# A 256-token, four-layer fp32 transformer kernel: the attention gates are applied after the last pair, and the delta rule's base inverse is computed by VectorE instead of GpSimd

## The reference, cut to what matters

```python
for l in range(DEPTH):
    h = rms_norm(x, norm_w[l])
    p = h @ w_in[l]
    qa, ka, va, za, ub, zb, qkv_c, b_c, a_c, zc = _split_cols(p)
    ...
    oa = sliding_window_sink_attention(qa, ka, va, sinks[l]) * jax.nn.silu(za)
    ob = conformer_conv_module(ub, ...) * jax.nn.silu(zb)
    oc = gated_deltanet(qkv_c, b_c, a_c, ...)
    oc = rms_norm(oc, c_onorm_w[l]) * jax.nn.silu(zc...)
    y = jnp.concatenate([oa, ob, oc], axis=-1)
    x = x + y @ w_out[l]
```

```python
lower = jnp.where(strict, jnp.einsum('bhnid,bhnjd->bhnij', kb, kc) * decay, 0.0)
sol = lax.linalg.triangular_solve(lower + eye, rhs, left_side=True, lower=True,
                                  unit_diagonal=True)
```

## Time and profile before

| | us |
|---|---|
| median of 3 runs | 3613.13 |
| lowest, highest | 3611.47, 3616.95 |
| profiled execution | 3615.81 |
| its span (first to last instruction) | 3614.0 |
| PE busy | 3472.0 (96%) |
| DVE busy | 2281.3 (63%) |
| ACT busy | 1851.8 (51%) |
| POOL busy | 155.6 (4%) |

### The profile page before, as it was taken

One profiled execution on the slowest core, in us unless ns is written; L12 is line 12 of the kernel. 1 busy time (PEld: TensorE's weight loads), 2 busy tenths in 40 slices (PEclk: granted clock), 3 DMA queues, 4 the chain that ended last, 5 costly groups with the idle time before them and its releaser, 6 DMA issues.

```text
span 3614.0 us, 41537 instructions
## 1 busy us (share of the span) xinstructions
PE 3472.0 (96%) x16074; PEld 2790.4 (77%) x16074; DVE 2281.3 (63%) x3126; ACT 1851.8 (51%) x2526; POOL 155.6 (4%) x243
## 2 busy tenths in 40 slices
PE   7988999988999999999999999999999999999998
PEld 5767778767778777788888888887777888888886
DVE  4956565966565656566666666656655566666665
ACT  4564555564555355655454454453566555445444
POOL 3014000013000000000000000000000000000000
PEclk9999999999999999999999999999999999999999
DMA  7434436434446345455655655653444565565564
GB/s 206 138 105 126 128 130 192 141 104 121 130 138 196 105 127 141 138 187 180 192 180 186 193 180 186 192 174 100 145 134 152 191 192 181 186 192 181 186 192 151
DMA packets 399092, 578.51 MB, mean 160 GB/s; under 512 B 25473, under 2 KB 222585, under 8 KB 398256
## 3 DMA queue, kind: packets, MB, share of 16 engines
q1 hardware_dynamic: 392544, 557.93, 50.4%
q0 software_dynamic: 5904, 16.75, 1.6%
q10 hardware_dynamic: 448, 1.18, 0.1%
HBM read 570.78 MB, written 4.98 MB: 159 GB/s over the span
## 4 chain that ended last, share of the span: by engine, by line
PE 82%; DVE 11%; ACT 4%; issue 2%; DMA 1%; DVEq 0%; ACTq 0%; SPq 0%
PE PS L706 79%; PE PS L703 3%; DVE WL L1844 3%; DVE ZA L2035 2%; ACT WH L1310 1%; DVE AR L1984 1%; DVE AR L2304 0%; ACT L1573 0%; DMA RAW<-in_w_in 0%; DVE SM L2243 0%; DMA X<-in_x 0%; DVE AR L2241 0%; ACT AR L1573 0%; ACT AR L1336 0%; ACT AR L1655 0%
## 5 line engine op out<-in xcount | busy, mean ns | idle before, releaser
L1844 DVE TENSOR_TENSOR WL<-RAW,WH 128x1024 fp32r<-128x1024 f32 x1056 | 1291.8, 1228 | 976.2 <-ACT WH L1310 973.6
L1310 ACT ACTIVATE WH<-RAW 128x1024 fp32r<-128x1024 f32 x1056 | 1105.1, 1056 | 965.6 <-PE PS L706 585.7
L706 PE MATMUL PS<-WH,Ah 128*128 128x512 f32 x3520 | 1431.9, 407 | 46.4 <-DVE WL L1844 32.9
L706 PE MATMUL PS<-WL,Ah 128*128 128x512 f32 x3520 | 1387.5, 394 | 0.0
L706 PE MATMUL PS<-WH,Al 128*128 128x512 f32 x3520 | 1387.4, 394 | 0.0
L706 PEld LDWEIGHTS PS<-WH,Ah 128*128 128x128 f32 x3520 | 671.9, 191 | 217.5 <-issue 40.8
L706 PEld LDWEIGHTS PS<-WL,Ah 128*128 128x128 f32 x3520 | 670.4, 190 | 145.4
L706 PEld LDWEIGHTS PS<-WH,Al 128*128 128x128 f32 x3520 | 672.3, 191 | 138.8 <-issue 6.8
L706 PE MATMUL PS<-WH,Zh 128*128 128x512 f32 x704 | 281.2, 399 | 0.0
L706 PE MATMUL PS<-WL,Zh 128*128 128x512 f32 x704 | 279.0, 396 | 0.0
L706 PE MATMUL PS<-WH,Zl 128*128 128x512 f32 x704 | 278.8, 396 | 0.0
(11 more groups left out here) (319 smaller groups left out, 2157.2 us busy)
## 6 DMA issues: line engine op xcount, KB each, us to landing
RAW<-in_w_in SPq DMA_DIRECT2D x368, 512.0 KB, 3.7
RAW<-in_w_up SPq DMA_DIRECT2D x704, 256.0 KB, 3.1
RAW<-in_w_down SPq DMA_DIRECT2D x176, 512.0 KB, 4.1
RAW<-in_w_out SPq DMA_DIRECT2D x64, 512.0 KB, 3.6
RAW<-in_w_o SPq DMA_DIRECT2D x64, 512.0 KB, 3.7
RAW<-in_w_in SPq DMA_DIRECT2D x64, 256.0 KB, 3.1
AR<-in_c POOLq DMA_DIRECT2D x2, 1600.0 KB, 7.6
AR<-bias_scratch POOLq DMA_DIRECT2D x16, 192.0 KB, 4.6
```

The source lines that it names most:

```text
L706: return T.matmul(o, lhs, rhs, start=start, stop=stop, skip_group_check=True)
L1310: act(WH[:, j % NW, 0:n], raw_view(j), ACT.Copy).then_inc(*w_hi())
L1844: tt(WL[:, j % NW, 0:w], raw_view(j), WH[:, j % NW, 0:w].bitcast(F32), SUB).then_inc(*w_lo())
```

## The change

1. The base's columns move from GpSimd to VectorE, three columns at each of ten steps of mixer c, directly after the tile's WL product and ahead of mixer a's work in the same step. The memset follows a step later. The DMAs and TTM's memset stay on GpSimd, which now waits for `one` from VectorE.
2. TensorE's pause ahead of the TTM transposes becomes 14 (from 12), ScalarE's 23 (from 20), VectorE's 1 + 10 + 5 (from 14).
3. Attention's `gt` no longer multiplies with the gate: it writes 0.5 times the result to OA, a part of tile AR. Step 3 waits for va alone. After step 14 the engines wait for va.z and za0, and VectorE multiplies GT by OA in two instructions (`gate0`, `gate1`: 128x512 and 128x1024), for which `merged` waits.
4. The chunks zb and za0 change places in the table.

```diff
-        ("za0", [(1280, 512)]), ("zb", [(3072, 512)])]
+        ("zb", [(3072, 512)]), ("za0", [(1280, 512)])]
...
-                for _ in range(12):
+                for _ in range(14):
                     yield
                 T.wait_ge(i_ttm, 64 * (l + 1))
...
-                        yield from e.until("va", "va.z", "za0")
+                        yield from e.until("va")
...
+                yield from e.until("va.z", "za0")
+                yield
                 e.flags.add("a")
...
-                for _ in range(12 + 8):
+                for _ in range(14 + 9):
                     yield
...
                 V.wait_ge(lower_in, 16 * (l + 1))
-                for _ in range(12 + 2):
-                    yield
+                yield
+                for j in range(1, 31):
+                    n = 31 - j
+                    t = BTMP[:, 0:j * n].rearrange("p (c i) -> p c i", i=n)
+                    if j > 1:
+                        V.wait_ge(*c_dve.at(m(f"add{j - 1}")))
+                    else:
+                        V.wait_ge(i_in, 16 * (l + 1))
+                    tt(t, BASE[:, 0:j, j:j + 1].broadcast_to([48, j, n]), BASE[:, j:j + 1, j + 1:32].broadcast_to([48, j, n]),
+                       MUL).then_inc(*c_dve(m(f"mul{j}")))
+                    V.wait_ge(*c_dve.at(m(f"mul{j}")))
+                    tt(BASE[:, 0:j, j + 1:32], BASE[:, 0:j, j + 1:32], t, ADD).then_inc(*c_dve(m(f"add{j}")))
+                    if j % 3 == 0:
+                        yield
+                V.memset(ZA[0:48, 3072:4096:33], 1.0).then_inc(*c_dve(m("one")))
+                yield
+                yield
+                yield
+                yield
+                yield
...
-                        gt = GT[:, h0 // 2, 128 * t:128 * t + 128]
                         V.wait_ge(*a_pe.at(m(f"pv{i - 3}")))
-                        stt(gt, bank(4 + (i - 3) % 4, 128), 0.5, gt, MUL, MUL).then_inc(*a_dve(m(f"gt{i - 3}")))
-                    yield
+                        ts(OA[:, h0 // 2, 128 * t:128 * t + 128], bank(4 + (i - 3) % 4, 128), 0.5, None, MUL).then_inc(*a_dve(m(f"gt{i - 3}")))
+                    yield
+                yield from e.until("va.z", "za0")
+                V.wait_ge(*a_dve.at(m("gt11")))
+                for i, (j, name) in enumerate(((4, "va"), (0, "za0"))):
+                    V.wait_ge(*e_dve.at(m(name + ".g")))
+                    gt = GT[:, j:j + 4 - 2 * (j // 4), :]
+                    tt(gt, gt, OA[:, j:j + 4 - 2 * (j // 4), :], MUL).then_inc(*a_dve(m(f"gate{i}")))
+                yield
                 e.flags.add("a")
...
-                G.wait_ge(i_in, 16 * (l + 1))
-                for j in range(1, 31):
...
-                G.memset(ZA[0:48, 3072:4096:33], 1.0).then_inc(*i_pool(m("one")))
-                G.wait_ge(*i_pool.at(m("one")))
+                G.wait_ge(*c_dve.at(m("one")))
+                G.wait_ge(*i_pool.at(l))
                 G.dma_start(base_scr[:, :, :], BASE).then_inc(i_out, 16)
```

## The result

| | median us | lowest, highest | executions |
|---|---|---|---|
| before | 3611.07 | 3605.66, 3617.03, and one of 12079.02 that only the median counts | 20 |
| after | 3619.85 | 3615.68, 3625.37 | 20 |

The ratio of the mean times, after to before, is 1.0025, with a 95% interval of 1.0018 to 1.0032: the change makes the kernel 9.0 us slower (6.5 to 11.6). The forecast was 3618.8, +5.7. The profiled execution of after took 3620.04 us, at its median; that of before, on which the forecast was built, took 3615.81, 4.7 above its median. That difference turns out to matter.

The account below looks back on a forecast made before the run. TensorE, busy 96%, was taken to bound the kernel, through its waits and clock. Layer 0: 4.3 + 3.7 − 3.3 − 2.9 = +1.8; layer 1 +3.9; together +5.7, giving 3618.8 us against the median 3613.13; range 3601 to 3630.

Parts of the forecast that it names:

- Columns: Ahead of qkv3's convolution: column operations on VectorE end TensorE's wait for the L1642 copies later, +4.3 us per layer.
- TTM: At the TTM transposes: loads arrive late, a new wait of 2.0 (layer 1: 2.8) plus 1.7 low clock, +3.7 and +4.5.
- The pauses: At the L2153 copies: the 2.1 wait and 1.7 low clock go, 0.5 returns at the predicated copies, −3.3 per layer.
- The pairs: In attention's pair loop and project start: 14.2 us go, 1.6 + 8.0 + 1.7 come, −2.9; layer 1 −1.6.
- Rival A: Pair loop doesn't bind: its 8.0 us of waits shrink to about 2, low clock goes, 3603.4 us; chance 0.23.
- Rival B: VectorE's columns arrive later: 0.25 us fixed per column operation instead of 0.18, 3628.8 us; chance 0.25.
- C: It cancels: column operations' fixed cost is 0.13 us, convolution 2.2 late, TTM wait 1.1, 3612.8 us; chance 0.15.
- my case: The main forecast with all terms as summed, 3618.8 us, its own range 3612 to 3626; chance 0.37.

Follow-up runs that it names:

- e2: Kernel before with only the columns moved to VectorE and the new pauses (14, 23, 16), gates and chunk order as before: 3616.81 us, 1.0015 of before.
- e4: The changed kernel run again unchanged, for a second profile: 3619.83 us, 1.0023 of before.
- e6: The changed kernel with one more pause ahead of the TTM transposes on all three engines (15, 24, 17): 3610.48 us, 0.9995 of before.
- e5: The changed kernel with the 30 columns left out on every engine, memset, transfers and pauses kept: 3600.14 us, 0.9966 of before.
- e10: Kernel before with only the new pauses (14, 23, 16): 3599.20 us, 0.9967 of before.
- e9: Kernel before with the new gates, chunk order and pauses, columns still on GpSimd: 3603.61 us, 0.9978 of before.
- e3: Kernel before with only the new gates and chunk order, columns on GpSimd and old pauses: 3606.78 us, 0.9988 of before.
- e1: Kernel before run again unchanged, for a second profiled execution: 3608.43 us, 0.9996 of before.
- e11: The changed kernel with the memset one step earlier, in the step of the last three columns: 3613.19 us, 1.0006 of before.

## Why the prediction was right, and where it was not

The time (3619.85) is in the range and 1.1 us from the forecast, and the move has the forecast's direction, +9.0 us for +5.7. That the time is so close is in part luck. The three executions of before on which the forecast stood had a median of 3613.13, twenty have 3611.07, and these 2.1 us make up for most of the 3.3 by which the move was forecast too small. In us the result is still within the prediction's bounds of "same" (3605.9 to 3620.4, chance 0.43); as a ratio, 1.0025, it is past 0.2% on the slower side (0.35). By its own steps:

**Columns: right in kind, near in size.** The ten places last 20.3 us for 21. TensorE passed the L1642 wait at 92.2 us after the conformer's wait in after, e2, e4 and e6, and at 87.2 to 89.3 in the five profiles with the columns on GpSimd. Against their mean of 88.4 this is +3.8 for +4.3; against the profile on which the forecast was built (89.3) it is +2.9. The sum had a slip of its own: 296.1 + 4.6 + 7.6 is 308.3, not 308.0, so the term should have been 4.6. The stretch from 277.20 was put at 10.8 us undisturbed and took 10.2 without the four places (278.10 to 295.91 in after). The key copies are part of that: they took 0.62 us where they had taken 1.50 beside GpSimd's columns. The Trainium skill (SBUF — State Buffer, Who interferes with whom) says that a copy can enter a mode that uses the port pair shared with GpSimd, and its sentence on instructions with a single input speaks only of those outside such modes. The trace agrees with that: with GpSimd idle the copies of 128 elements take 0.155 us each, less than the 0.20 from one undisturbed product of that size to the next, and beside GpSimd's columns 0.375 (1.50 for four).

**TTM: the wait right, its low clock not always there.** The waits were 2.14, 2.61 and 3.21 in layer 0 (after, e2, e4) and 3.8 to 4.0 in layer 1, for 2.0 and 2.8. The memset came at 323.59 for 324.2 (1.9 us early if both are counted from the conformer's wait, since the convolution was early too), but the way from there was 0.7 to 1.7 us longer in layer 0 and 1.5 to 1.8 in layer 1, since GpSimd's store took longer (below). The 1.7 us of low clock behind it came in layer 1 of e2 and e4 only. All in all the columns cost 17 us by the runs; the terms gave 2 × 4.3 + 3.7 + 4.5 = 16.8. Errors inside (an earlier convolution, a longer way, less low clock) cancelled, which is luck. And e5 corrects the reason: the wait for TTM is set by the number of tiles between memset and transposes, not by how late VectorE is.

**The pauses: mis-sized.** The term was −3.3 per layer, −6.6; measured alone −11.9 (e10), and on top of the gates −3.6 (e9 − e3). The wait for L2153 went as said and nothing came back at the predicated copies, where I had put 0.5. What I put elsewhere belongs here: pair 0's wait falls from 1.85 to 1.13 because the pairs begin a tile later and va's transposes fall into it, and 0.33 at zc's transposes goes. In all, the waits of the two stretches are 30.1 us in e10 against 36.2 and 37.3 in the two profiles of before, 6 to 7 of the 11.9. The rest I put to clock that falls in some executions of before and has less occasion to fall here: the clock loss is 13.3 against 25.4 and 12.0.

**The pairs: the term that fails once the pauses are there.** The term was −2.9 and −1.6, together −4.5. Alone the gates measure −4.3 (e3); with the pauses in place they measure +4.0 (e9 − e10) or +2.9 (e4 − e2). In layer 0 of after the waits that came were about as forecast: 1.15 at va's transposes, 2.11 at pair 4's scores (forecast 1.9), 1.53 + 0.39 behind the zb gate (1.7), 1.41 + 0.20 at the end (1.6). Those at pair 3 were 0.33 twice for 1.0, and those at pairs 5 to 7 (0.9, 0.8, 0.6) are missing. In after TensorE itself lost 3.3 us to the clock behind pair 4, which gives VectorE time, but e4 lost only 1.7 there and doesn't wait at these pairs either, so their absence is not explained. The loop's waits were 5.8 us instead of 8.0, the clock loss 5.0 instead of 1.7. The larger mistake is on the side of before. I set 14.2 us against them, 7.6 of it low clock read in one profiled execution as if every execution had it. The same stretch of layer 0 in e1 has 6.9 us of waits and 5.0 of low clock, 11.9. With 11.9 the term would have been −0.6 (after's profile has 7.5 + 5.0), and in layer 1, 6.9 + 3.6 in e1 stand against 6.2 + 5.1 in after: +0.8. For layer 1 the prediction also took over layer 0's 3.0 of low clock at pair 0, and so counted 6.3 where the first profile itself has 4.9.

With the pauses taken first and the gates on top, two terms were wrong in opposite directions, by 5 and by 8 us. In the other order the gates are −4.3 for −4.5, and the pauses on top −3.6 for −6.6. So the runs don't say which of the two terms is wrong. They say that the two don't add: the gates are worth −4.3 alone and +4.0 beside the pauses. The prediction summed them as independent and took low clock of one execution off in both. That the sum came out only 3 us low is luck as far as this goes. Rival A (the loop does not bind) is refuted by the 2.1 us waits, though the loop's 5.8 us lie between its 2 and my 8.0. Rival B (0.25 us fixed) is refuted by operations of 0.18. C's condition (0.13 fixed) isn't met either. The median landed between my case and B's.

## What to carry to other kernels

Before a low-clock stretch is entered in a sum, look whether it is there in a second execution: waits repeated to 0.2 us here (one to 0.4), the clock behind them did not, and 13 us hung on it. When a change brings counted pauses along, measure the pauses alone; here they were worth 12 us by themselves (4 beside the gates) and hid the cost of the move, 17 us, that they came with. An idle share of 37% on an engine is no room for 20 us of work per layer if the work stands ahead of something that TensorE waits for, in the one stretch where that engine is full.

## What the runs showed of the hardware

**The same store took 1.3 us longer beside a full weight stream.** From the store's row to the row of the loads that wait for it, with the columns on GpSimd (e10) and without any (e5), at the same time from the start:

```profile
310.97 0.55 POOL L2552 DMA_DIRECT2D base_scratch<-ZA  x1 [0.29 <-POOL ZA L2550]
314.06 2.47 POOL L2556 DMA_DIRECT2D AR<-base_scratch  x4 [2.54 <-DMA base_scratch<-ZA]
```

```profile
310.96 0.53 POOL L2560 DMA_DIRECT2D base_scratch<-ZA  x1 [54.34 <-DVE ZA L2152]
315.31 2.48 POOL L2564 DMA_DIRECT2D AR<-base_scratch  x4 [3.83 <-DMA base_scratch<-ZA]
```

These are 3.09 and 4.35 us for the same 192 KB. The windows over them, e10's 311–314 and then e5's 311–315.3 (last: clock, DMA share, GB/s):

```profile
311.00:314.00 3.00, 2.73 (x9) 2.37 (x10) 2.15 (x3) 2.62 (x4) 0.52 (x1) 0.50 0.29 66
```

```profile
311.00:315.30 4.30, 4.30 (x20) 3.56 (x20) 2.09 (x2) 1.75 (x2) 0.49 (x1) 1.00 0.80 211
```

In the kernels with the columns on GpSimd the base happened to be finished while TensorE stood still for the L1642 copies, and with it the weight loads. With the columns on VectorE, or gone, the store shares the transfer engines with a full stream: 3.05 to 3.21 us against 4.24 to 4.48 in the profiles of layer 0, and 3.95 against 5.2 to 5.4 in layer 1. An exception is e11 (3.56 and 4.37, at DMA shares of 0.92 and 0.95), so it may also depend on where between two weight tiles the store falls. Nor was it the 54 to 66 us for which GpSimd had been idle: in e11 these were 65. The contention is read from the windows and not shown; no run varied it alone, and in every slower case it is also VectorE, not GpSimd, that writes the memset ahead of the store.

**The clock behind a wait does not follow from the length of the wait.** The same 2.06 us for L2153 was followed by 0.50 in one execution and 1.00 in the other, 3.50 for L1642 by 0.50 (310 to 314 us) and 3.34 by 1.00 (310.8 to 314). In after, 2.14 for TTM was followed by 1.00, 2.11 at pair 4 by 0.57 (425 to 433).
